# Hybrid pooling and RWKV-7 trunk on one core: key square and decay difference on other engines, solve and low-rank products in 64x64 quarters

## The reference

```python
pf = pf + (token_shift(pf) - pf) * mu
r, k, v, wd, ad = the columns of pf
w_log = -softplus(-(w0 + tanh(wd) @ w_lora_up)) - 0.5
decay = exp(-exp(w_log))
a = sigmoid(a0 + ad @ a_lora_up)
kk = k * k_k
kk = kk * rsqrt(sum(kk * kk, per head) + 1e-12)
k = k * (1.0 + (a - 1.0) * k_a)
# a = -kk, b = kk * a; state S (64 x 64 per head)
S_t = S_(t-1) diag(w_t) + (S_(t-1) a_t) b_t^T + v_t k_t^T
y_t = S_t r_t
```

## Time and profile before

| | |
|---|---|
| median of 3 runs | 2628.68 us (2628.33 to 2629.49) |
| the profiled execution | 2628.31 us, its span 2626.6 us |
| granted clock of TensorE, mean | 0.988 |
| busy: PE, DVE, ACT, POOL | 2547.5, 1520.5, 1163.3, 484.0 us |
| inverse steps (L1004) begin | 788 us after the span's start, with block 0 |

### The profile page before, as it was taken

How to read it: one execution, slowest core, us unless ns; L and a number is a source line. 1 busy time by engine, 2 the same in 40 slices (tenths; PEclk the granted TensorE clock), 3 DMA queues, 4 the chain that set the end, 5 groups by cost and what they waited for, 6 DMA issues and landing times.

```text
span 2626.6 us, 74898 instructions
## 1 busy us (share of the span) xinstructions
PE 2547.5 (97%) x30741; PEld 2102.5 (80%) x30741; DVE 1520.5 (58%) x3199; ACT 1163.3 (44%) x2626; POOL 484.0 (18%) x622
## 2 busy tenths in 40 slices
PE   6999999999999999999999999999999999999995
PEld 6777777777778888888888888888888888888883
DVE  2412121212157677777767777776677777667774
ACT  3324242323225455544445554454455445445542
POOL 3210101010121112211211121121112112111210
PEclk8999999999999999999999999999999999999997
DMA  8632322323210001000000101000010100001000
GB/s 338 255 112 81 110 93 99 102 90 112 81 65 10 26 29 39 26 34 26 26 26 26 42 26 34 26 26 26 26 42 26 34 26 26 26 26 42 26 18 25
DMA packets 68706, 153.08 MB, mean 58 GB/s; under 512 B 3977, under 2 KB 37342, under 8 KB 66398
## 3 DMA queue, kind: packets, MB, share of 16 engines
q1 hardware_dynamic: 63134, 130.08, 14.1%
q0 software_dynamic: 1680, 11.01, 1.0%
q10 hardware_dynamic: 3632, 7.87, 0.8%
HBM read 98.61 MB, written 50.33 MB: 57 GB/s over the span
## 4 chain that ended last, share of the span: by engine, by line
PE 74%; DVE 16%; ACT 4%; issue 3%; DMA 1%; DVEq 0%; SPq 0%; ACTq 0%
PE banks L949 20%; PE banks L355 16%; PE banks L984 9%; PE banks L387 8%; PE banks L932 7%; PE banks L1004 6%; DVE SM L1587 2%; DVE LA L1570 2%; DVE LA L1576 2%; PE banks L960 1%; PE banks L1112 1%; DVE t L1467 1%; DVE mix L1438 1%; DVE kk L1474 1%; DVE stmp L1519 1%
## 5 line engine op out<-in xcount | busy, mean ns | idle before, releaser
L949 PE MATMUL banks<-xT,w 128*128 128x128 f32 x5232 | 634.0, 279 | 0.0
L949 PEld LDWEIGHTS banks<-xT,w 128*128 128x128 f32 x5232 | 598.3, 192 | 31.1 <-issue 27.1
L1255 ACT ACTIVATE LX<-banks 128x512 f32<-128x512 f32 (+1 forms) x384 | 184.9, 524 | 642.6 <-DVE WT L1532 436.5
L355 PE MATMUL banks<-xT,w 128*128 128x256 f32 x2048 | 448.3, 381 | 4.8 <-ACT xT L475 4.8
L355 PEld LDWEIGHTS banks<-xT,w 128*128 128x128 f32 x2048 | 391.3, 191 | 65.3 <-issue 10.5
L932 PE MATMUL banks<-xT,w 128*64 128x128 f32 x6944 | 420.1, 274 | 0.0
L932 PEld LDWEIGHTS banks<-xT,w 128*64 128x64 f32 x6944 | 380.3, 137 | 6.3
L984 PE MATMUL banks<-wo,Y 128*128 128x512 f32 x512 | 234.3, 601 | 4.7 <-DVE Y L1492 4.7
L387 PE MATMUL banks<-wo,yc 128*128 128x512 f32 x512 | 224.8, 592 | 0.0
L672 DVE TENSOR_SCALAR gate<-gate 128x1024 f32<-128x1024 f32 x16 | 11.1, 694 | 367.7 <-ACT gate L495 367.7
L1532 DVE TENSOR_TENSOR WT<-banks,level_mask 128x256 f32<-128x256 f32 x256 | 102.6, 422 | 187.7 <-PE banks L1004 179.7
(11 more groups left out here) (185 smaller groups left out, 3587.6 us busy)
## 6 DMA issues: line engine op xcount, KB each, us to landing
x_in<-in_x SPq DMA_DIRECT2D x16, 1024.0 KB, 7.4
xr<-in_x SPq DMA_DIRECT2D x32, 512.0 KB, 4.3
xt_dram<-xT SPq DMA_DIRECT2D x32, 512.0 KB, 8.6
h_dram<-xr SPq DMA_DIRECT2D x32, 512.0 KB, 2.6
xT<-xt_dram SPq DMA_DIRECT2D x32, 512.0 KB, 3.3
gate_row<-h_dram SPq DMA_DIRECT2D x32, 512.0 KB, 4.3
out<-gate_row SPq DMA_DIRECT2D x32, 512.0 KB, 2.6
w<-in_w_in POOLq DMA_DIRECT2D x8, 1088.0 KB, 10.9
```

The source lines that it names most:

```text
L355: last = nc.tensor.matmul(bank[t // 2][:, (t % 2) * T1:(t % 2 + 1) * T1], w1[:, k, t * P:(t + 1) * P], xT[:, k, :], start=(k == 0), stop=( ...
L949: last = (by_halves if halves else nc.tensor.matmul)(bank[b][:, q * P:(q + 1) * P], w2[:, k, (t0 + q) * P:(t0 + q + 1) * P], xT[par][:, k, :],
L1255: s(nc.scalar.activation(to, of, ACT.Copy), lx_ready, hold=False)
```

## The change

The square of the key moves from GpSimd to ScalarE (`key_square`) and stands there behind `sigmoid(0)`, which itself moves ahead of `second_values`; `sigmoid(1)` moves ahead of `key_scale`. The difference G - sig moves from GpSimd to VectorE (`decay_ahead`). On VectorE, `decay_sum` moves ahead of `take_r(1)`, `clamp(1)` ahead of `new_state`, and `replaced_key` is split in two, with the last `shift` between its parts. `state_sum` waits for the state update alone (`s_ps`), and the wait for Y moves to the update of the state. `low_rank` issues 16 products of 64x64 instead of 8 of 64x128. `solve` issues its 8 products in four quarters instead of two; for this, the heads of odd pairs lie in the other partition half in AI and R, and the result lies in two PSUM banks. AI is made in four operations a chunk in place of two. A wait for `y_ready` now stands ahead of the second solve. The diff (without a hunk that adds a blank line):

```diff
--- before.py
+++ after.py
@@ -60,7 +60,7 @@
 LV = len(LEVELS)
 STEPS = LV + 2
 HEAD_DVE = 9
-DVE_OWN = 14
+DVE_OWN = 18
 LN_MAX = 1e19
 
 
@@ -955,11 +956,13 @@
                 def low_rank():
                     nx.wait(mix_ready, 1)
                     nx.wait(th_ready, 1)
+                    let_through(pe, pe_gate)
+                    of = (th[0:LORA, :], mix[LORA:P, 12, :])
                     for p in range(NP):
-                        for i, (part, rhs) in enumerate(((slice(0, LORA), th[0:LORA, :]), (slice(LORA, P), mix[LORA:P, 12, :]))):
-                            last = nc.tensor.matmul(bank[2 + i][:, p * P:(p + 1) * P], up[part, p * P:(p + 1) * P], rhs,
-                                                    start=True, stop=True)
-                            if p == NP - 1:
+                        for i, c in QUARTERS:
+                            last = nc.tensor.matmul(bank[2 + i][half(c), p * P:(p + 1) * P], up[half(i), p * P + c * HD:p * P + (c + 1) * HD],
+                                                    of[i], start=True, stop=True)
+                            if p == NP - 1 and i != c:
                                 last.then_inc(lora_ps.sem, 1)
 
                 def key_norm():
@@ -1031,18 +1034,21 @@
                         s.wait(bt_ready, 2)
                     for p in range(NP):
                         for e in range(2):
-                            last = nc.tensor.matmul(bank[5][half(e), p * HD:(p + 1) * HD], LA[e][:, p, j, 0], SV[e][:, p],
+                            last = nc.tensor.matmul(bank[5][half(e ^ p % 2), p * HD:(p + 1) * HD], LA[e][:, p, j, 0], SV[e][:, p],
                                                     start=True, stop=True)
                     last.then_inc(r_ps.sem, 1)
 
                 def solve(j):
 
                     s.wait(r_ready, j + 1)
+                    if j:
+                        s.wait(y_ready, j)
                     let_through(pe, pe_gate)
-                    for p in range(NP):
-                        for e in range(2):
-                            h = half(e)
-                            last = nc.tensor.matmul(bank[5][h, 256 + p * HD:256 + (p + 1) * HD], LX[h, p // 2, j, p % 2, 0], R[h, p], start=True, stop=True)
+                    for a in range(2):
+                        for r, c in QUARTERS:
+                            x = r ^ c
+                            last = nc.tensor.matmul(step_banks[1][half(c), x, 256 + a * HD:256 + (a + 1) * HD], LX[half(r), a, j, x, 0],
+                                                    R[half(r), 2 * a + x], start=True, stop=True)
                     last.then_inc(u_ps.sem, 1)
 
                 def state_and_output(j, first=False):
@@ -1214,6 +1220,10 @@
                     hd(nc.scalar.activation(sig[:, i], sig[:, i], ACT.Ln, bias=1.0), ln_own)
                     hd(nc.scalar.activation(sig[:, i], sig[:, i], ACT.Exp, scale=-1.0), sig_ready)
 
+                def key_square():
+                    hd.wait(kk_ready, 1)
+                    hd(nc.scalar.activation(rn[:, :, :], kk[:, :, :], ACT.Square), kk2_ready, hold=False)
+
                 def key_scale():
                     hd.wait(norm_ps, 1)
                     hd(nc.scalar.activation(rn[:, :, :].rearrange(flat), bank[4][:, :], ACT.Ln, bias=eps[:, 1:2]))
@@ -1254,10 +1264,13 @@
                             to, of = LX[:, a, :, :, 0], step_banks[a][:, :, 0:P].rearrange("p j (q t) -> p j q t", q=2)
                         s(nc.scalar.activation(to, of, ACT.Copy), lx_ready, hold=False)
 
+                def update_of(e):
+                    return step_banks[1][half(e), :, 256:256 + 2 * HD].rearrange("p x (a t) -> p x a t", a=2)
+
                 def take_u(j):
                     s.wait(u_ps, j + 1)
-                    s(nc.scalar.activation(UV[j][0][half(0), :, :].rearrange(flat), bank[5][half(0), 256:512], ACT.Copy), act_half, hold=False)
-                    s(nc.scalar.activation(UV[j][1][half(1), :, :].rearrange(flat), bank[5][half(1), 256:512], ACT.Copy), u_ready)
+                    s(nc.scalar.activation(UV[j][0][half(0), :, :].rearrange("p (a x) t -> p x a t", x=2), update_of(0), ACT.Copy), act_half, hold=False)
+                    s(nc.scalar.activation(UV[j][1][half(1), :, :].rearrange("p (a x) t -> p x a t", x=2), update_of(1), ACT.Copy), u_ready)
 
                 def second_values(to):
                     for e in range(2):
@@ -1314,15 +1327,16 @@
                     take_u(0)
                     if ahead:
                         exp_low_rank(1)
+                        sigmoid(0)
+                        key_square()
                     s.wait(y_ps, 1)
                     second_values(SV)
                     if not first:
                         pv.wait(out_ps, 2)
                     take_y(0)
                     if ahead:
-                        sigmoid(0)
+                        sigmoid(1)
                         key_scale()
-                        sigmoid(1)
                     take_u(1)
                     if ahead:
                         decays()
@@ -1364,10 +1379,6 @@
 
                 def head(n):
                     hd.block(n)
-                    hd.wait(kk_ready, 1)
-                    hd(nc.gpsimd.tensor_tensor(rn[:, :, :], kk[:, :, :], kk[:, :, :], ALU.mult), kk2_ready)
-                    hd.wait(G_ready, 1)
-                    hd(nc.gpsimd.tensor_tensor(egx[:, :, :], G[:, :, :], sig[:, 0], ALU.subtract), gprev_ready)
                     hd.wait(k2_ready, 1)
                     hd.wait(exps_ready, 1)
                     for e in range(2):
@@ -1460,6 +1471,9 @@
                     hd(nc.vector.tensor_tensor_scan(G[:, :, :].rearrange(flat), restart[:, :], sig[:, 0].rearrange(flat), 0.0,
                                                     ALU.mult, ALU.add), G_ready)
 
+                def decay_ahead():
+                    hd(nc.vector.tensor_tensor(egx[:, :, :], G[:, :, :], sig[:, 0], ALU.subtract), gprev_ready, hold=False)
+
                 def new_key():
 
                     hd.wait(sig_ready, 2)
@@ -1468,12 +1482,14 @@
                     hd(nc.vector.tensor_tensor(k2[:, :, :], mix[:, 4:8, :], t2[:, :, :], ALU.mult), k2_ready)
                     hd(nc.vector.tensor_tensor(rk[:, :, :], mix[:, 0:4, :], k2[:, :, :], ALU.mult), rk_ready)
 
-                def replaced_key():
+                def taken_key():
 
                     hd.wait(rn_ready, 1)
                     hd(nc.vector.tensor_tensor(kk[:, :, :], kk[:, :, :], rn[:, :, :], ALU.mult))
                     hd(nc.vector.scalar_tensor_tensor(out=t2[:, :, :], in0=kk[:, :, :], scalar=-1.0, in1=sig[:, 1],
                                                       op0=ALU.mult, op1=ALU.mult))
+
+                def decayed_key():
                     hd.wait(exps_ready, 1)
                     for e in range(2):
                         h = half(e)
@@ -1513,7 +1529,7 @@
                     s(nc.vector.tensor_copy(R[:, :, :].rearrange(flat), bank[5][:, 0:256]), r_ready)
 
                 def state_sum(j):
-                    s.wait(y_ps, j + 1)
+                    s.wait(s_ps, j + 1)
                     for e in range(2):
                         h = half(e)
                         s(nc.vector.tensor_tensor(stmp[h], per_head(bank[7][h, 0:256]), SV[e][h], ALU.add),
@@ -1564,6 +1580,7 @@
                     hd.block(n + 1)
                     if not first:
                         pv.block(n - 1)
+                        pv.wait(y_ps, NC)
                     s.wait(exps_ready, 2)
                     for e in range(2):
                         h = half(e)
@@ -1589,9 +1606,10 @@
                                                       gram_mask[:, :].unsqueeze(1).broadcast_to([P, NP, P]), ALU.mult), sm_ready)
                         for e in range(2):
                             h = half(e)
-                            s(nc.vector.tensor_tensor(AI[h, :, j, :, 0], SM[j][e][h, :, 0].rearrange("q (a p) t -> q a p t", a=2),
-                                                      ident64[h, :].unsqueeze(1).unsqueeze(1).broadcast_to([HD, 2, 2, HD]), ALU.add),
-                              hold=bool(e and j))
+                            for x in range(2):
+                                s(nc.vector.tensor_tensor(AI[half(e ^ x), :, j, x, 0], SM[j][e][h, :, 0].rearrange("q (a x) t -> q a x t", a=2)[:, :, x],
+                                                          ident64[h, :].unsqueeze(1).broadcast_to([HD, 2, HD]), ALU.add),
+                                  hold=bool(e and j and x))
                     first_factor()
                     if not first:
                         group_scale(1 - par)
@@ -1627,17 +1645,21 @@
                         key()
                         clamp(0)
                     state_sum(0)
+                    if ahead:
+                        clamp(1)
+                    s.wait(y_ps, 1)
                     new_state(0, s, s_ready)
                     if ahead:
```

(7 more changed lines are left out.)

## The result

The changed kernel takes 2640.8 us (median of 5 runs, 2640.5 to 2645.0), the kernel before 2628.9 beside it: a ratio of 1.0048, 95% interval 1.0036 to 1.0060. It is 12 us slower where 11 us less were forecast. The profiled execution took 2643.4 with a span of 2641.7, 2.6 above the median, so sizes read from its first and last blocks are somewhat high.

A forecast was written before the change was run, and what follows sets the result against it. PE, busy 97%, was taken to bound it, with waits for ACT and DVE. Solve -0.22, Gram wait -0.35, AI +0.21 make -0.36 a block; over thirty blocks -10.8 us, 2628.3 to 2617.5; range 2605 to 2634.

The forecast's parts named there:

- rival 2: Square comes late: first clamp's 1.27 is not contention, key norm starts 0.75 late; +0.39 a block, 2640; chance 0.06.
- Solve in quarters: PE's solves: four rounds instead of eight save 0.23 each; second solve booked at 0.22, first worth nothing behind ACT.
- The bank rule: Different row tiles cannot access one PSUM bank together; as rival 4, no gain from solve, -0.14 a block, 2624, chance 0.05.
- The square: Key square on ACT: ready for PE at about 64.3, needed for the key norm at 64.36; price 0 to 0.15, taken as 0.
- AI pieces: AI on DVE in eight operations, 0.29 each, four at 0.31 take 1.24; 0.69 more a block, bounds 0.46 to 1.77.
- rival 1: Small AI operations on DVE are dear: at 0.42 and the gap, E is 1.77, +0.72 a block, 2650; chance 0.12.
- The wait before the Gram products: PE's wait for DVE's last LA product goes; gain 0.35 a block on average.
- the term from the Gram start to the inverse step: Gram start to first inverse step becomes 8.02 on average, 0.21 longer than 7.81, as earlier DVE pays most of AI.
- the decay difference to DVE, and DVE's new order: Adds 0.69 to DVE, yet LA is ready at 77.8, so the Gram wait goes, with 1.2 to spare.
- rival 5: GpSimd contention just moves: BK overlaps other DVE work, LA late again; 1.2 us of room first; inside the forecast's spread.
- low-rank products in quarters: 16 quarter products cost what 8 halves cost, ahead of the ACT-bound update: zero; bounds 0.1 below, about 0.05 above.
- block 0: First block pays for AI under GpSimd's traffic, perhaps 1; the last gains as much on its bare solves.

The follow-up runs named there:

- most of the contention gone: Changed kernel with low-rank halves and mended prologue, three quarters of GpSimd's half of BK left out from block 1 on: 2618.4 against 2632.7 with all of BK.
- the clean pair: Kernel before with moved square, moved difference and new orders, no quarters: 2611.0; the same with block 0's key square ahead of the prologue's exponentials: 2606.2.
- the quarter solve alone: Changed kernel with low-rank products back in halves and block 0's key square ahead of the prologue's exponentials: 2632.7 (1.0015).
- moves: Kernel before with the moved square, the moved difference and the new queue orders, and neither kind of quarters: 2611.0 (0.9929).

## Why the prediction was wrong

The time lay outside the range, on the side that got 0.14. It fell near the 2640 of rival 2, but by chance: that rival's late square did not happen in the loop, and its clamp takes 0.43.

**Right.** *Solve in quarters* keeps its pace: 0.41 and 0.46 busy, second solve to update 0.13 to 0.22 shorter (0.22 booked). The bank rule did not bite: both row halves write into the same two banks at full pace. The first solve is worth nothing (from the from-state products to the update 4.30 before, 4.29 after), with a wait of 0.50 where 0.4 was said. *The square* comes in time in the loop (update to key norm 3.17 before and after), although the queue of ACT was added up 0.16 too short (64.9 and 3.91 make 68.81, not 68.65). *AI pieces*: 0.287 each, four in 1.24, just as worked out; rival 1 is out. *The wait before the Gram products* is gone: from the second update to the Gram start it took 10.45 before and 9.91 after, a gain of 0.54 where 0.35 was booked.

**Wrong, first: the term from the Gram start to the inverse step, +0.21 a block ("1.27 + 6.06 + 0.69 = 8.02").** It was +0.67 without the slow branch (8.62 even, 8.33 odd) and +0.84 with it. Its 6.06 and 0.69 held (from SM's start to the inverse step an odd block takes 6.71, and 5.97 and 0.69 make 6.66); the 1.27 did not, because of the part before it, "the decay difference to DVE, and DVE's new order". That part said LA would be ready 8.9 after the second update (68.93 to 77.8), "with 1.2 to spare". It is ready 9.8 after it (1520.42 to 1530.20), because L1489, put where GpSimd's BK runs, takes 1.65. That was rival 5, which I left inside the spread since "1.2 us of room must go first". The room was counted to the Gram products only. Behind LA stand the new state, dend and the bonus, 1.74 in all, before SM; SM could start 1.27 after the Gram start only if DVE's queue was through by then, and that left 0.8. Besides, the 0.72 between transposes and Gram in block 0 was itself a wait for LA (ready 0.05 before they started); free it is 0.52, which used up 0.2 of the room. The 0.6 that was left is less than the 0.96: SM started 1.62 after the Gram start (1531.94 less 1530.32). So of the sum of -0.36 a block nothing was left: without the slow branch the even blocks are at +0.05 and the odd ones at -0.11. With most of the contention gone the kernel is at 2618.4. That this is close to the forecast is in part luck: low-rank quarters and the prologue's fault were out of that kernel too.

**Wrong, second: "low-rank products in quarters", priced at zero with bounds of 0.1.** They came 0.17 faster to the solve (1.09 to 0.92), and ACT covered that, as the zero assumed; whether a change of mode was saved no run shows. But 16 more products in the loop body made the back-edge branch go from 0.36 to 2.1, 4.9 us here and 6 alone. In the trace of before the branch took 0.36 and I did not look at it, and I never asked what the change does to the length of a queue's program.

**Wrong, third: the prologue was left out.** The step of the square was worked out for the loop. The same function stands in the prologue behind other instructions, and cost PE 2.8 us and the clock some more: 4.8 us by the clean pair.

**Fourth, a size: block 0.** I said perhaps 1 for AI under GpSimd's traffic. The two groups of four take 1.69 and 2.66 there and PE waits 3.35 before the inverse step:

```profile
785.80 1.69 DVE L1610 TENSOR_TENSOR AI<-SM,ident 64x128 f32<-64x128 f32 x4
788.98 2.66 DVE L1610 TENSOR_TENSOR AI<-SM,ident 64x128 f32<-64x128 f32 x4
```

```profile
794.05 1.99 PE L1007 MATMUL banks<-AI,W 64*64 64x128 f32 x32 [3.35 <-DVE W L1560]
```

Behind this wait the inverse step ran in 1.99 instead of 1.10 in this execution, at a mean clock of 0.77 from 786 to 801; in that of the quarter solve alone the same wait of 3.35 was followed by 1.10. So block 0 takes 52.6 or 55.1, where it took 51.7 before.

The balance of the 12 us: moves -19, solve in quarters +25 (2611.0 to 2635.9, two sets; 14 of it go with the contention), low-rank quarters +5 (2635.9 to 2640.8), 11 in all. The 4.8 of the prologue is inside the -19. How much of the -19 each move and each new order gives was not tried.

**Not foreseen either: the last block.** From the first to the last inverse step block 31 takes 19.97 before, 23.24 in the changed kernel and 22.0 to 23.2 with every other version that squares on ACT. Most of it is one wait in ACT's queue, before the copy ahead of the last step, first before, then changed:

```profile
2585.96 0.38 ACT L1255 ACTIVATE LX<-banks 128x256 f32<-128x256 f32 x1 [2.69 <-DVE WL L1560]
```

```profile
2601.73 0.66 ACT L1265 ACTIVATE LX<-banks 128x256 f32<-128x256 f32 x2 [5.01 <-issue]
```

In the changed kernel DVE's first part of WL is ready at 2599.4 and the copy starts 2.3 later, with nothing in the profile that it waits for. All twelve versions with the square on ACT show this wait at the same copy (2.3 to 2.6), the two with the square on GpSimd do not (0.04). What sets it off was not tried. The other 0.9 lies in eight products of the output projection (4.95 at a mean granted clock of 0.74 before, 5.86 at 0.63 changed). Over the whole stretch it is 0.72 in both kernels. In the next 23 us it is 0.50 in the changed kernel and 0.68 before, but what is left is not longer (39.5 and 40.1 us to the end).

## What to carry to other kernels

A step that is moved must be placed beside what runs on the other engines at its new place, and the room it uses must be counted to the end of the queue that sets the next wait, not to the first one. Look at every copy of an order (prologue, loop, last block), and at the length of the program around a loop: sixteen more small products a turn, which cost nothing on the array, made its branch slow. When a change is made of several parts, each is worth its own run; here the cheap part (-23) was hidden by the dear one.

## What the runs showed of the hardware

- A loop's back-edge branch on PE took 0.36 us in eight programs of this study (the kernel before among them) and 1.4 to 2.7 in six others, whose blocks were longer by 8 products (32 records of matmul and weight load), or by 30 semaphore increments and nothing else.
- An operation of VectorE with two SBUF inputs that ran beside a product on GpSimd took 1.65 us (128x512, L1489) or 1.17 (64x512, BK and LA) in place of 0.69. One that met only the last 0.17 us of the first product (L1488) took 0.72. Shifts and state sums, with one input in PSUM, kept their times beside it.
- Sixteen records of the solve in four quarters, with both row halves writing into each of two banks, took 0.41 to 0.46; in two quarters they took 0.68.
- After PE had stood still for about 3 us, the mean granted clock was sometimes 0.77 to 0.90 over the next 15 to 17 us, sometimes 1.00 (0.77 and 1.00 behind the same wait of 3.35).
- One copy on ACT in the last block started 2.3 to 2.6 us after its last input was ready in all twelve versions with one more activation a block on ACT, and after 0.04 in the two without.
